# Sampled bursts, store waits, gate weights and shift rows moved in a hybrid decoder step on one core

## The reference, cut to what matters

```python
h = _rms(x) * (1 + scale[:, None, :]) + shift[:, None, :]
z = h @ w_in
q_a, k_a, v_a, gate_a, q_b, k_b, v_b, f_b, gate_b, m_a, m_b = jnp.split(
    z, np.cumsum(_SIZES)[:-1].tolist(), axis=-1)
...
y_a = (o_a.reshape(B, T, W_A) * jax.nn.silu(gate_a)) @ w_out_a
y_b = (o_b.reshape(B, T, W_B) * jax.nn.silu(gate_b)) @ w_out_b
y = (jax.nn.sigmoid(m_a) * y_a + jax.nn.sigmoid(m_b) * y_b) @ w_o
```

## Time and profile before

| | us |
|---|---|
| median of 3 runs | 2597.69 |
| lowest and highest | 2593.37, 2602.4 |
| the profiled execution, its own time | 2602.89 |
| its span | 2601.3 |
| PE, DVE, ACT, POOL busy | 2487.1, 1584.4, 901.2, 187.4 |
| mean granted clock of PE | 0.981 |

### The profile page before, as it was taken

How to read it: one execution, slowest core, us unless ns; L and a number is a source line. 1 busy time by engine, 2 the same in 40 slices (tenths; PEclk the granted TensorE clock), 3 DMA queues, 4 the chain that set the end, 5 groups by cost and what they waited for, 6 DMA issues and landing times. The chain is left out here.

```text
span 2601.3 us, 34432 instructions
## 1 busy us (share of the span) xinstructions
PE 2487.1 (96%) x12851; PEld 1986.3 (76%) x12851; DVE 1584.4 (61%) x2603; ACT 901.2 (35%) x1433; POOL 187.4 (7%) x182
## 2 busy tenths in 40 slices
PE   5899999999999989999999999999999987999998
PEld 2688888887788878878888778877777754888886
DVE  3321235653676417777887588977878656655554
ACT  4011112225232217775001456644444433222121
POOL 0000012210132100000000200000000000000000
PEclk8999999999999999999999899999999998999999
DMA  8454455546455467774455866445557297544341
GB/s 297 164 214 174 162 169 172 156 153 220 132 168 134 142 216 194 171 181 114 139 141 148 200 147 147 95 80 121 100 117 164 65 329 277 176 129 129 129 132 52
DMA packets 286709, 413.12 MB, mean 159 GB/s; under 512 B 77995, under 2 KB 170507, under 8 KB 277004
## 3 DMA queue, kind: packets, MB, share of 16 engines
q1 hardware_dynamic: 274378, 377.91, 51.3%
q10 hardware_dynamic: 11132, 33.17, 3.5%
q0 software_dynamic: 1056, 0.13, 0.1%
HBM read 273.62 MB, written 137.52 MB: 158 GB/s over the span
## 5 line engine op out<-in xcount | busy, mean ns | idle before, releaser
L1734 DVE CUSTOM_DVE_ANT_0 max_s_ps<-max_s_ps,max_causal 128x128 f32<-128x128 f32 (+7 forms) x256 | 194.2, 768 | 74.9 <-PE max_s_ps L1791 55.6
L708 PE MATMUL proj_z<-first_km,h_hi 128*128 128x512 f32 x576 | 229.7, 399 | 0.0
L708 PE MATMUL proj_z<-first_km,h_lo 128*128 128x512 f32 x576 | 226.1, 393 | 0.0
L708 PE MATMUL proj_z<-first_v,h_hi 128*128 128x512 f32 x576 | 224.5, 390 | 0.0
L2114 ACT ACTIVATE att_b_pf<-att_b_s_ps 128x1024 f32<-128x1024 f32 (+2 forms) x160 | 142.5, 897 | 111.9 <-PE att_b_s_ps L2171 88.3
L1693 ACT ACTIVATE max_s_ps<-max_s_ps,max_neg_top 128x128 f32<-128x128 f32 (+2 forms) x192 | 161.1, 840 | 52.0 <-DVE max_neg_top L1734 32.7
L2131 DVE TENSOR_TENSOR att_b_p_lo<-att_b_pf,att_b_p_hi 128x1024 fp32r<-128x1024 f32 (+2 forms) x160 | 170.5, 1065 | 5.5
L1737 DVE TENSOR_REDUCE max_neg_top<-max_s_ps 128x1 f32<-128x1024 f32 x128 | 154.2, 1224 | 25.6 <-PE max_s_ps L1791 19.1
L708 PE MATMUL proj_z<-proj_w_hi,h_hi 128*128 128x512 f32 x384 | 151.7, 395 | 0.0
L708 PE MATMUL proj_z<-proj_w_hi,h_lo 128*128 128x512 f32 x384 | 149.8, 390 | 0.0
L708 PE MATMUL proj_z<-proj_w_lo,h_hi 128*128 128x512 f32 x384 | 149.6, 389 | 0.0
(11 more groups left out here) (438 smaller groups left out, 6132.8 us busy)
## 6 DMA issues: line engine op xcount, KB each, us to landing
w_raw<-in_w_in SPq DMA_DIRECT2D x144, 256.0 KB, 3.8
smp_v_a<-scratch_mixes SPq DMA_DIRECT2D x16, 1024.0 KB, 4.8
map_qm<-scratch_q_hi SPq DMA_DIRECT2D x48, 256.0 KB
map_k<-scratch_k_hi SPq DMA_DIRECT2D x37, 256.0 KB
head_w<-in_w_ada SPq DMA_DIRECT2D x8, 1024.0 KB, 7.5
scratch_mixes<-proj_out SPq DMA_DIRECT2D x32, 256.0 KB, 2.6
scratch_k_hi<-proj_v_hi SPq DMA_DIRECT2D x32, 256.0 KB, 2.4
scratch_k_lo<-proj_v_lo SPq DMA_DIRECT2D x32, 256.0 KB, 2.9
```

The source lines that it names most:

```text
L708: ins = nc.tensor.matmul(out, left(*lt), right(*rt), start=first and n == 0, stop=last and n == len(terms) - 1)
L1734: nc.vector.tensor_tensor_reduce(s, s, causal[:, 1024 - w:1024], -1.0, -NEG, ALU.add, ALU.min, accum_out=neg_top[:, kh, u, qt:qt + 1]).the ...
```

## The change

Four edits. In `project(k, 1)` burst 0 moves behind tile (0, 0) and burst 1 behind tile (0, 2), and ACT takes them after its tiles 1 and 3. The waits for the second projection's stores move from SP's end of that stage into the joint stage, where SP, ACT, DVE and POOL each wait first (PE doesn't), and their semaphores are kept until then. The joint stage's gate weights are loaded two pieces a tile in the first four tiles of a chunk. The stores of the shift rows move from ACT's round 46 to 45, and their reads from round 47 to 46. For `project(k, 0)` the waits stay where they were.

```diff
--- before.py
+++ after.py
@@ -95,7 +95,7 @@
                     retire(k)
                     gate_buffers(k, c2)
                     project(k, 1)
-                    retire(k, kept=k.gate_w.loaded)
+                    retire(k, kept=k.gate_w.loaded + [done for done, _ in k.proj_stored])
                     raw.close()
                     att_buffers(k, c3)
                     gates_and_maxima(k)
@@ -847,6 +847,12 @@
         sp.dma_start(k.bias_row[part].rearrange("(g r) p -> r g p", g=2), f.rows[part][:].bitcast(F32)).then_inc(f.stored, 16)
 
 
+def proj_ended(k, eng):
+
+    for done, count in k.proj_stored:
+        eng.wait_ge(done, count)
+
+
 def project(k, half):
 
 
@@ -873,7 +879,7 @@
     def burst_behind(c, j):
 
         if half:
-            return {(0, 0): 1, (c, HALF - 1): c + 2}.get((c, j), NS)
+            return {(0, 0): 0, (0, 2): 1, (c, HALF - 1): c + 2}.get((c, j), NS)
         return {(0, 0): 0, (0, 4): 1, (c, HALF - 2): c + 2}.get((c, j), NS)
 
     def rows_of(j):
@@ -1083,14 +1089,13 @@
                             load_w(NM + c + 2, kt, slice(col, col + 512))
                 if half == 0:
                     later_weights(k, later, sp)
-                for s in range(R):
-                    sp.wait_ge(stored[s], 16 * seen[s])
-                for s in range(2):
-                    sp.wait_ge(parts_stored[s], 32 * len(range(s, len(parts_index), 2)))
-                    sp.wait_ge(v_stored[s], 32 * len(range(s, len(v_index), 2)))
+                k.proj_stored = [(stored[s], 16 * seen[s]) for s in range(R)]
+                k.proj_stored += [(parts_stored[s], 32 * len(range(s, len(parts_index), 2))) for s in range(2)]
+                k.proj_stored += [(v_stored[s], 32 * len(range(s, len(v_index), 2))) for s in range(2)]
                 if half:
-                    sp.wait_ge(bias.stored, 80)
+                    k.proj_stored.append((bias.stored, 80))
                 else:
+                    proj_ended(k, sp)
                     sp.wait_ge(side.stored, (2 * POS + 1) * 16)
                     sp.wait_ge(later.raw_loaded, 16 * KD)
                     for i in range(2):
@@ -1136,8 +1141,6 @@
                             sampled_kept(q)
                 for i in range(NM // 2):
                     mixes(i)
-                if half:
-                    sampled_kept(0)
                 for n, (c, j, kind, b) in enumerate(tiles):
                     pn = rows_of(j)
                     src = z[0:pn, n % R, :]
@@ -1185,8 +1188,8 @@
                         forget_rows_high(k, bias, act, ps_f)
                     if n - BEHIND in parts_index and not turned_first(n):
                         turned_high(act, n - BEHIND)
-                    if half and (c, j) == (0, 1):
-                        sampled_kept(1)
+                    if half and n in (1, 3):
+                        sampled_kept(n // 2)
                     if half and j == HALF and c + 2 < NS:
                         sampled_kept(c + 2)
                 if half == 0:
@@ -1320,8 +1323,6 @@
                         pe.wait_ge(w_loaded[kt], 16 * (q + 1))
                     sampled_burst(k, pe, s_bank(q), w_raw).then_inc(s_done, 1)
 
-                if half:
-                    burst(0)
                 for g, cols in enumerate(f_cols):
                     at = slice(0, cols.stop - cols.start)
                     for kt in range(KD):
@@ -1643,6 +1644,7 @@
             @block.gpsimd
             def _(pool):
                 clear_retired(k)
+                proj_ended(k, pool)
                 nc.gpsimd.memset(causal[:], 0.0).then_inc(zeroed, 1)
                 pool.wait_ge(zeroed, 1)
                 nc.gpsimd.affine_select(out=causal[:, 1024 - P:1024], in_=causal[:, 1024 - P:1024], compare_op=ALU.is_ge, fill=NEG,
@@ -1664,10 +1667,11 @@
                             sp.wait_ge(s_done, free)
                         (load_max_q if what == "q" else load_max_k)(k, sp, x)
                         ahead += 1
-                    if c + 1 < len(gw.chunks) and j < KD:
+                    if c + 1 < len(gw.chunks) and 2 * j < KD:
                         if c and j == 0:
                             sp.wait_ge(z_done, c * T)
-                        load_gate_w(k, sp, c + 1, j)
+                        for kt in range(2 * j, 2 * j + 2):
+                            load_gate_w(k, sp, c + 1, kt)
                     if n == NZ - TAIL:
                         assert ahead == len(loads) and upto[n - 1] == NT_
                         sp.wait_ge(s_done, NT_)
@@ -1694,6 +1698,7 @@
                                          accum_out=sums[:, kh, u, qt:qt + 1]).then_inc(sum_done, 1)
 
                 x = 0
+                proj_ended(k, act)
                 for n in range(NZ):
                     if n:
                         copy(n - 1)
@@ -1714,11 +1719,10 @@
                     if n == NZ - TAIL + 1:
                         act.wait_ge(turned, 1)
                         nc.scalar.activation(rows[HI][:], s_ps[:, 0:2 * P].rearrange("p (g c) -> p g c", g=2), ACT.Copy).then_inc(hi_done, 1)
-                    if n == NZ - TAIL + 2:
                         act.wait_ge(lo_done, 1)
                         for part in range(2):
                             act.dma_start(k.neg_max[part].rearrange("(g r) p -> r g p", g=2), rows[part][:].bitcast(F32)).then_inc(shift_stored, 16)
-                    if n == NZ - 1:
+                    if n == NZ - 2:
                         act.wait_ge(shift_stored, 32)
                         for g in range(TILES // GROUP):
                             load_q(k, act, 0, g, shift_only=True)
@@ -1738,6 +1742,7 @@
                                             negate=True).then_inc(max_done, 1)
 
                 x = 0
+                proj_ended(k, dve)
                 dve.wait_ge(causal_made, 1)
                 for n in range(NZ):
                     while x < upto[n]:
```

## The result

The changed kernel takes 2585.34 us in the median of 6 runs (2582.85 to 2591.85), against 2598.18 for the kernel before in as many (2593.37 to 2602.4): 12.8 us less. The ratio that is worked out from all runs is 0.9946, with an interval of 0.9933 to 0.9959. It is not the quotient of the two medians (0.9951), and taken alone it would mean 14.0 us, within 10.7 and 17.4. The prediction said 2583.7, so faster, as forecast, by 14.0; by the medians it is 12.8. The profiled execution has a span of 2582.9 against 2601.3.

The account below looks back on a forecast made before the run. PE, busy 96% of the span, was taken as the bound, losing time where it idles or runs at its lower clock. Gains of 0.7 + 1.0 + 8.6 + 3.7 = 14.0 us took the 2597.7 median to 2583.7, range 2576 to 2594.

Parts of the forecast that it names:

- A: Second projection: sampled bursts moved behind tiles 0 and 2; gain 0.7 us, bounds gain 1.2 and loss 2.0.
- The covers that I costed: Second projection: after the move, DVE's weight split keeps 1.8 us to spare and burst 1's weight loads 1.9.
- meet the same slow stretch: Second projection's start: forget products, now first, run at 1.2 GHz as burst 0 did, so no 1.7 us gain.
- B: Joint stage's start: store waits moved out of the projection's end block; gain 1.0 us, bounds 0.6 and 3.0.
- the middle term: Joint stage's start: last gate piece lands 3.5 us after issue, so PE starts at 965.2, gain 1.0.
- C: Joint stage: gate weights two pieces a tile remove waits of 0.88 and 5.10 us and 2.6 of slow clock; gain 8.6.
- Rival 3 (score banks): Joint stage gives nothing back, since scores wait for score banks; 5.4 us left, 2592.3 us; 12%.
- rival 4 (late map loads): Joint stage: added gate loads push map loads past their use, PE waits and slows; 2606.7 us; 6%.
- D: attention_a's start: shift rows' stores go out 4.8 us earlier, their reads earlier too; gain 3.7 us, between 0 and 4.1.
- one microsecond more: Before attention_a: allowance for the fuller queue in the landing of the shift rows' stores, then at 1439.1.
- rival 2: attention_a's start: D gives nothing because the reads land with SP's loads; 10.3 us in all, 2587.4 us; 13%.
- Rival 1 (the clock holds, 27%): attention_a's start: with idle down to 2.1 us the clock stays high; 3 us more, 2580.7 us; 27%.

Follow-up runs that it names:

- forget-first kernel: The kernel before with burst 0 moved behind the second projection's forget products, still ahead of tile 0; burst 1 as before: 2599.82 us, one run.
- D alone: The kernel before with only the shift rows' stores and reads one round earlier: ratio 0.9995 (0.9985 to 1.0005).
- with B: The kernel before with only the second projection's store waits moved into the joint stage: ratio 1.0003 (0.9993 to 1.0013).
- C alone: The kernel before with only the joint stage's gate weights loaded two pieces a tile: ratio 0.9961 (0.9949 to 0.9973).
- A alone: The kernel before with only the sampled bursts and their copies moved behind tiles 0 and 2: ratio 0.9991 (0.9981 to 1.0001).
- the last of these kernels: The changed kernel with chunk 0's gate weights two a tile and query group 3 held back until the maxima's stores landed: 2580.82 us, ratio 0.9926.
- the early pieces: The changed kernel with chunk 0's gate weights loaded two a tile in the second projection's last chunk: 2584.92 us, ratio 0.9942.

## Why the prediction was right, and where it was wrong

**A (0.7 predicted).** The certain part is the wait, 0.9: 4.02 to 3.14, and 3.13 or 3.14 in all eight kernels that hold A. The covers that I costed held. Burst 1 follows its tile at 679.83 without idle time; its weights had landed in 4.6 us where I took 5.8. That a lost cover is dear is what the forget-first kernel shows. Not borne out was the sentence that the forget products "meet the same slow stretch". From PE's start to the rise of the clock it is 2.8 to 3.6 us in the nine kernels that begin with forget products; in the four that begin with burst 0 it is 5.5 and 5.6 in two (before, D alone), but 2.7 and 2.6 with B and with C alone. So from PE's stop to the first turn it is 33.5 to 33.8 with A, and 35.59 and 35.63 or 34.30 and 33.71 without (the 33.71 of C alone is short because PE stopped some 0.5 late there). Of the 2.1 us between this pair, 1.2 comes from the length of that stretch; whether the order of the work shortens it, or luck did, is not shown. A alone is worth 2.3 us with an interval from slightly below 0 to 4.9.

**B (1.0 predicted).** The mechanism was right: block 967 no longer releases PE, the last gate piece is late next, as the middle term said. The size was off: I let the piece land 3.5 us after its issue, as a 64 KB store had. It was issued at 957.10 and PE started at 961.14, so a 256 KB piece took 4.0. With 0.6 the gain came out at the lower of my bounds; against the other kernels without B (7.41 to 7.84 idle) it is between 0.1 and 0.6. As priced, the moved waits cost nothing measurable.

**C (8.6 predicted, 9.2 measured).** Right term by term: 0.88 and 5.10 are gone, the clock is 1.00 across the old slow stretch, and the rest is within what such a stretch varies. It is 10.1 of the total by its own timing, the only part whose interval excludes no change. Rival 3 (score banks) and rival 4 (late map loads) would have shown as idle time in the joint stage, and there is none.

**D (3.7 predicted, 0.5 measured).** This is the step that failed. Its first term was right: against PE's stop the first store goes out 4.8 us earlier, as said, and the second 5.3. The landing of the second, "one microsecond more", was 1.6 (12.0 after 10.4). The failing term is the next one: reads at their old 4.3 us. They took 7.5, since they now went out while more of SP's q loads was still to be moved; the first ACT packets after them stand in the window from 1430 on, and PE starts as SP's queue runs out. 5.3 - 1.6 - 3.2 = 0.5. That is rival 2, to which I had given 13%; I had set it aside because the earlier trace rows showed ACT's packets alternating with SP's. The rows were right and my reading too wide: they showed a queue that had started, not how long it takes to start. By the rule of the Trainium skill that I weighed there (DMA: Bandwidth & Descriptors, Queues, rings and completion order), the increments come no earlier than SP's earlier writes. The result agrees with what that forecast for D. Whether increments alone were also held cannot be told, as the packets were late already.

The 4.3 us was no latency of the reads to begin with. Before the change, too, PE started when SP's queue ran out. SP's queue before (its timeline), and the queue rows of 1446 to 1447 us, in which SP's packets all but end:

```profile
1420.36 1.30 SPq L1481 DMA_DIRECT2D map_k<-scratch_k_hi  x2
...
q10 hardware_dynamic: 113, 0.20, 67.6%
q1 hardware_dynamic: 33, 0.05, 22.8%
```

and SP's queue after:

```profile
1406.06 1.30 SPq L1482 DMA_DIRECT2D map_k<-scratch_k_hi  x2
```

From the issue of k2, the first of SP's 5 MB, to PE's start it is 26.8 us before (1420.36 to 1447.14) and 26.2 after (1406.06 to 1432.30). It is 26.6 to 27.1 in the kernels with A, with B and with C alone and in the forget-first kernel, 26.2 with D alone. So SP's 5 MB set PE's start in both, whenever ACT's reads went out, and the 0.5 that D won is this difference. With the last 0.75 MB held back PE starts 23.7 us after k2 (1408.41 to 1432.06): SP's backlog is the cause. The sign stood in the earlier trace rows, a DMA share of 1.04 until 1446.

**Rival 1 (the clock holds, 27%)** was never met on its own terms, since no kernel brought the idle time down to 2.1. The clock fell in every kernel: with 5.26 us idle, but also with 2.75, 2.67, 2.62 and 2.41, and with the last two only after PE had started again.

C came out 0.6 better and A up to 1.4 better than priced, B 0.4 and D 3.2 worse: the error of the sum, 1.2 to 1.6, is smaller than D's alone because A's and C's went the other way. That the total came so close is luck in this sense; what was foreseen is C, the greater part of it.

## What to carry to other kernels

Before a dependent transfer is moved earlier, look at what the other queue has outstanding at the new time: a small store and read-back issued on ACT here took 12.0 and 7.5 us behind SP's large loads, and 2.0 for the store with that queue empty. Hurrying the small one won 0.5 us of idle time here; holding back the last of the large loads took 2.6 us off it (5.26 to 2.67). That this shows in the time of the kernel is likely only in the last of these kernels, not shown. And a two-a-tile load that moves the last piece some tiles ahead of its use is cheap insurance when PE is the bound: here the two waits that this removed and the slow clock behind the second were worth more than all the other edits together.

## What I had not expected of the hardware

- ACT's queue moved no packet from 1412 to 1417 and from 1426 to 1430 while SP's loads were queued. After the first of these stretches it shared one for one. Where its transfers wait in that time the trace doesn't show, and I leave it open.
- After attention_a's start PE runs at 1.2 GHz for 10 to 13 us in every kernel although it is busy throughout (1.00 in the windows), whereas at the joint stage the low stretch is 3.7 us long from PE's start in the changed kernel and 3.4 with the early pieces, and at the second projection 2.6 to 5.6. Its length doesn't follow the idle time ahead: 10.4 us low after 5.26 idle, 13 after 2.75, 10.2 after 2.41. What in attention_a's products keeps it low I did not try.
- At the joint stage with 3.62 us idle, the clock fell only at 959.2, 4.3 after PE's stop and after PE had started again (0.61 in the microsecond from 959). Here the fall came late, and a short wait was paid for by the work behind it.
